# A hybrid attention layer: the gate chain moved into the output product, scores in half precision, the value projection in two pieces

## The reference

```python
u = rmsnorm(h, norm_g)
proj = u @ w_in            # gq 256, gk 256, gv 512, g_gate 512, g_low 16, sq 512, sk 128, sv 128, s_gate 512
z = g_low @ w_gate_up + b_gate
log_a = log_sigmoid(z) / 16
# gated linear attention, 4 heads (dk 64, dv 128): S_t = diag(exp(log_a_t)) S_{t-1} + k_t v_t^T ; o_t = q_t S_t
o_gla = rmsnorm(o, gla_norm)
# sliding-window attention: 8 heads, 2 key heads, width 64, window 128
s = (q . k) * 64**-0.5 ; p = softmax([s where in the window, sink])[:-1] ; o_swa = p @ v
y = concat(o_gla * silu(g_gate), o_swa * silu(s_gate)) @ w_out
h = h + y ; y_prompt = rmsnorm(h, norm_f)
```

## Time and profile before

| | |
|---|---|
| median of 3 runs | 963.65 us (963.21 to 964.19) |
| the profiled execution | 962.79 us, its span 960.8 us |
| granted PE clock over the span | 0.957 |
| PE busy | 889.7 us, 93% of the span |
| DVE, ACT, POOL busy | 72%, 42%, 6% |
| chain that ended last | PE 73%, DVE 21%, issue 2%, ACT 2% |

### The profile page before, as it was taken

The page is one execution under the profiler, slowest core; times in us unless marked ns, Lnnn a source line. Parts: engine busy times, 40 slices in busy tenths (PEclk is TensorE's granted clock), DMA queues, the critical chain, the costliest instruction groups (busy, mean ns, idle before and its releaser), DMA issues.

```text
span 960.8 us, 21676 instructions
## 1 busy us (share of the span) xinstructions
PE 889.7 (93%) x8701; PEld 618.8 (64%) x8701; DVE 689.4 (72%) x2140; ACT 399.4 (42%) x1096; POOL 57.6 (6%) x101
## 2 busy tenths in 40 slices
PE   1697699999999999999999999999999999999977
PEld 1673457585857666675758585766767575856755
DVE  5999858586776859495867678594959585776673
ACT  6885434343534243343434342434434343433311
POOL 0000101010101001010101010000101010101000
PEclk9798699999999999999999999999999999997776
DMA  9640102020202010010202020201102020101220
GB/s 381 249 166 0 67 1 89 1 90 1 89 1 89 2 66 24 23 67 2 89 1 90 1 89 2 89 1 42 49 4 86 1 89 1 48 2 45 78 113 24
DMA packets 15219, 56.47 MB, mean 59 GB/s; under 512 B 3569, under 2 KB 5001, under 8 KB 13840
## 3 DMA queue, kind: packets, MB, share of 16 engines
q1 hardware_dynamic: 14832, 55.02, 15.3%
q10 hardware_dynamic: 288, 0.07, 0.0%
HBM read 44.30 MB, written 10.78 MB: 57 GB/s over the span
## 4 chain that ended last, share of the span: by engine, by line
PE 73%; DVE 21%; issue 2%; ACT 2%; DMA 1%; SPq 0%; DVEq 0%
PE bank L511 19%; PE bank L512 19%; PE bank L513 19%; DVE flex L1404 4%; PE bank L661 3%; DVE bank L1398 2%; PE bank L595 2%; DVE flex L406 2%; PE bank L708 2%; PE bank L685 1%; PE bank L681 1%; DMA w_out_lo<-in_w 1%; DVE flex L1309 1%; PE bank L647 1%; DVE flex L405 1%
## 5 line engine op out<-in xcount | busy, mean ns | idle before, releaser
L511 PE MATMUL bank<-u_hi,w_in_hi_lo 128*128 128x128 f16 (+1 forms) x1288 | 208.8, 215 | 12.6 <-DVE w_in_hi_lo L1546 12.3
L512 PE MATMUL bank<-u_lo,w_in_hi_lo 128*128 128x128 f16 (+1 forms) x1288 | 208.4, 215 | 0.0
L513 PE MATMUL bank<-u_hi,w_in_hi_lo 128*128 128x128 f16 (+1 forms) x1288 | 208.4, 215 | 0.0
L511 PE MATMUL bank<-w_in_hi_lo,u_hi 128*128 128x512 f16 (+3 forms) x528 | 177.2, 344 | 0.8 <-issue 0.6
L512 PE MATMUL bank<-w_in_hi_lo,u_hi 128*128 128x512 f16 (+3 forms) x528 | 176.9, 343 | 0.0
L513 PE MATMUL bank<-w_in_hi_lo,u_lo 128*128 128x512 f16 (+3 forms) x528 | 176.8, 343 | 0.0
L511 PEld LDWEIGHTS bank<-u_hi,w_in_hi_lo 128*128 128x128 f16 x1288 | 124.2, 99 | 24.7 <-DVE w_in_hi_lo L1546 12.5
L512 PEld LDWEIGHTS bank<-u_lo,w_in_hi_lo 128*128 128x128 f16 x1288 | 124.2, 99 | 0.2
L513 PEld LDWEIGHTS bank<-u_hi,w_in_hi_lo 128*128 128x128 f16 x1288 | 124.2, 99 | 0.0
L511 PE MATMUL bank<-w_out_hi,ogT_hi 128*128 128x512 f16 x256 | 98.0, 383 | 0.0
L512 PE MATMUL bank<-w_out_lo,ogT_hi 128*128 128x512 f16 x256 | 97.9, 382 | 0.0
(11 more groups left out here) (263 smaller groups left out, 1765.3 us busy)
## 6 DMA issues: line engine op xcount, KB each, us to landing
xT<-in_xT SPq DMA_DIRECT2D x16, 512.0 KB, 4.5
x_rows<-in_xq SPq DMA_DIRECT2D x16, 512.0 KB
flex<-in_w SPq DMA_DIRECT2D x4, 2048.0 KB, 9.9
flex<-in_xq SPq DMA_DIRECT2D x16, 512.0 KB, 3.5
out_y<-flex SPq DMA_DIRECT2D x16, 512.0 KB, 2.6
w_out_lo<-in_w SPq DMA_DIRECT2D x2, 2048.0 KB, 9.9
w_out_hi<-in_w SPq DMA_DIRECT2D x1, 2048.0 KB, 10.2
w_out_hi<-in_w SPq DMA_DIRECT2D x1, 1088.0 KB, 7.2
```

Of the source, the lines that this page charges most:

```text
L511: nc.tensor.matmul(out, a_hi, b_hi, start=start and i == 0, stop=False)
L512: nc.tensor.matmul(out, a_hi, b_lo, start=False, stop=False)
L513: mm = nc.tensor.matmul(out, a_lo, b_hi, start=False, stop=stop and i == last)
```

## The change

1. The gate chain of the next tile (turn_low, gate_up, take_low, take_z, log_gate, sums, differences, decays, factors) is done in the body of the tile before. turn_low(t) and gate_up(t) in PE's body now serve tile t+1: turn_low stands after turn_keys, gate_up before gla_out. On DVE take_z follows take_gv, sums follow norm_x, factors stand between residual and final_norm. On ACT log_gate follows head_norm, decays stand after the gates and before split_u. Tile 0 has functions of its own at the start, in bank accS.
2. The scores are three half-precision products. ACT writes q's high half (take_sq), DVE the low half (a new take_sq, which now frees the bank), DVE both halves of k (take_kv, one operation more), all scaled by 2^-15; the scale of the scores moves into the constant `nsig` of row_max. The copy of k to the next tile's window copies both halves.
3. gv's projection is cut: four of its eight steps after sklow, four after leaf_scores. split_v moves behind sums.

The place of bc(t+2) is the same in both lists. The diff, cut to its core:

```diff
         tr = Ring(...
-                  [("glT", "act"), ("z", "dve"), ("pt0", "dve"), ("pt1", "dve"), ("pt2", "dve"), ("pt3", "dve"),
-                   ("KST", "act"), ("SU", "dve"), ("og0", "dve"), ("og1", "dve")])
+                  [("pt0", "dve"), ("pt1", "dve"), ("pt2", "dve"), ("pt3", "dve"), ("KST", "act"),
+                   ("glT", "act"), ("z", "dve"), ("SU", "dve"), ("og0", "dve"), ("og1", "dve")],
...
             def scores(t, pair):
                 for i in range(2):
-                    for h, name in enumerate(units):
-                        mm = nc.tensor.matmul(..., sq[r:r + HD, t.p, 2 * pair + i, :], kwin[r:r + HD, t.p, :],
-                                              start=True, stop=True)
+                    for step, (lq, lk) in enumerate(((0, 0), (0, 1), (1, 0))):
+                        for h, name in enumerate(units):
+                            mm = nc.tensor.matmul(..., q16[r:r + HD, t.p, lq, 2 * pair + i, :],
+                                                  k16[r:r + HD, t.p, lk, :], start=step == 0, stop=step == 2)
...
             def body(t):                      # PE
-                    turn_low(t)
                     proj(nxt, "gqk")
-                    gate_up(t)
                     scores(t, 0)
                     proj(nxt, "sq")
                 turn_probs(t, 0)
...
                 scores(t, 1)
                     proj(nxt, "sklow")
+                    proj(nxt, "gv", 4)
                 values(t, 0)
...
-                    proj(nxt, "gv")
+                    proj_rest(nxt, "gv", 4)
                 values(t, 2)
...
                 turn_keys(t)
+                turn_low(t)
                     proj(nxt, "gg", 3)
+                gate_up(t)
                 gla_out(t)
...
             def body(t):                      # ACT
-                    take_low(t)
                     take_qk(nxt)
-                log_gate(t)
                 probs(t, 0)
...
-                decays(t)
                 probs(t, 2)
...
                 take_kst(t)
+                take_low(t)
...
                 head_norm(t)
+                log_gate(nxt)
                 take_out(t, 0)
...
                 nc.scalar.preload_act_table_set(LOG_EXP_SET)
+                decays(nxt)
                     split_u(t + 2)
...
             def take_kv(t):                   # DVE
-                    V.tensor_scalar(kwin[:, t.p, P:2 * P], bank[:, 0:P], inv[:, 2:3], None, ALU.mult)
+                    V.tensor_scalar(k[:, 0, P:2 * P], bank[:, 0:P], V_UNIT, None, ALU.mult).then_inc(dve_k.sem, 1)
...
+                    V.scalar_tensor_tensor(out=k[:, 1, P:2 * P], in0=bank[:, 0:P], scalar=V_UNIT,
+                                           in1=k[:, 0, P:2 * P], op0=ALU.mult, op1=ALU.subtract)
...
+            def take_sq(t):
+                act_q.wait(dve, "qh", t)
+                V.scalar_tensor_tensor(out=q16[:, t.p, 1], in0=pj.bank("sq", t)..., scalar=V_UNIT,
+                                       in1=q16[:, t.p, 0], op0=ALU.mult, op1=ALU.subtract
+                                       ).then_inc(pj.freed["dve"], 1)
...
                 if i == 3:                    # DVE, start
...
+                    V.tensor_scalar(nsig[:, :], invq[:, 1:2], inv[:, 2:3], -1.0 / (V_UNIT * V_UNIT), ALU.mult, ALU.mult
+                                    ).then_inc(scored, 1)
+                    dve.wait_ge(scored, 1)
+                    V.tensor_scalar(nsig[:, :], nsig[:, :], -SCORE_FLOOR, None, ALU.min)
...
+                if i == 3:
+                    take_sq(Tile(0))
                 if i == 4:
+                    take_sq(Tile(1))
                     take_gv(Tile(0))
...
             def body(t):                      # DVE
-                    take_z(t)
                     row_max(t, 0)
                     row_max(t, 1)
-                sums(t)
+                    take_sq(nxt)
                 take_pt(t, 0)
...
-                factors(t)
                 take_pt(t, 2)
...
                     take_gv(nxt)
-                    split_v(nxt)
+                take_z(t)
...
                     norm_x(t + 2)
+                sums(nxt)
+                    split_v(nxt)
                     scale_u(t + 2)
                     split_u(t + 2)
                 residual(t)
+                factors(nxt)
                 final_norm(t)
...
+            differences(Tile(0))              # POOL
             def body(t):
-                differences(t)
                 gates_over_sums(t)
+                differences(t + 1)
```

More of the change, by code:

```diff
@@ L113, with __init__ @@
 class Ring:
-    def __init__(self, banks, full, freed, order, tail=None, head=None):
+    def __init__(self, banks, full, freed, order, tail=None, head=None, last=None):
         self.banks, self.full, self.freed, self.order = banks, full, freed, order
+        self.last = order if last is None else last
         self.tail = order if tail is None else tail
@@ L125, in _list @@
     def _list(self, t):
+        if t.static and t.off == NT - 1:
+            return self.last
         return self.tail if t.sample else self.order
@@ L610, in values @@
             def values(t, u):
[L611 to L612 removed]
+                if u == 0:
+                    if t.static and t.off == 0:
+                        pe.wait_ge(z_taken, 1)
+                    else:
+                        dve_o.wait(pe, "sg", t + -1)
                 if u == 0:
@@ L637, in gate_up, with first_turn_low, first_gate_up @@
                 mm.then_inc(tr.full, 1)
+            def first_turn_low():
+                pj.wait_freed(pe, "sklow", Tile(0))
+                nc.tensor.transpose(accS[0:RANK, 0:P], glow[:, 0, :], ident[:, :]).then_inc(low_turned, 1)
+            def first_gate_up():
+                pe.wait_ge(low_taken, 1)
+                for f in range(FT):
+                    mm = nc.tensor.matmul(accS[:, (f + 1) * P:(f + 2) * P], wgu[:, f * P:f * P + P], glT[:, :],
+                                          start=True, stop=True)
+                mm.then_inc(z_full, 1)
             def leaf_scores(t):
@@ L825, in _ @@
             proj(Tile(0), "gv")
-            turn_low(Tile(0))
+            first_turn_low()
             proj(Tile(1), "gv")
@@ L830, in _ @@
             pe.wait_ge(init, 1)
-            gate_up(Tile(0))
+            first_gate_up()
             scores(Tile(0), 0)
@@ L1734, in _ @@
                     dve.wait_ge(w_lo_done, i)
-                    take_z(Tile(0))
+                    first_take_z()
                     row_max(Tile(0), 0)
```

112 lines of the change are left out of this document (75 added, 37 removed).

## The result

The kernel after takes **952.43 us** (median of 4 runs, 950.77 to 952.50), the kernel before 963.76 on the same chip: ratio 0.9879, 95% interval 0.9862 to 0.9896. It is 1.2% faster, 6.2 us dearer than the 946.2 forecast, and inside the range of 941 to 956. The profiled execution took 952.36 us with a span of 950.6, so 1.8 us lie around the span, where it was 2.0 before.

The account below looks back on a forecast made before the run. PE was taken to bound the kernel, busy 51.57 of 52.29 us a tile. Bodies -19.3, start +3.4 and end -1.5 summed to -17.4, giving 946.2 us, range 941 to 956.

Parts of the forecast that it names:

- The gap: PE's wait for ACT's exponentials at transposes 2 and 3, bodies 1 to 14: closes, -0.93 x 14 = -13.0 us.
- The scores: A call of twelve half-precision products, heads side by side: 0.80 us, -0.27 a call, 28 times, -7.6 us.
- The first rival: No overlap of the two heads in float16 scores: a call takes 1.43 us, total 964; chance 10%.
- The switches: Changes in the number of rows between PE's products: one more a tile at 0.09 us, +1.3 us.
- (b): Row maxima 0 and 1 behind factors: probabilities fit by 0.2 us, costed nothing; T is the tile's start on PE.
- second rival: Exponentials late again, at the first transposes: 0.5 x 14 = 7 us, total 953; chance 15%.
- (a): u for the tile after next, across DVE, POOL and ACT: ready T+49.9, wanted T+50.9, covered by 1.0 us.
- (c), (d): Leaf bank freed T+23.0, wanted T+23.4; take_z holding DVE until gate_up ends, T+28.7: both costed at nothing.
- The start: Before tile 1: gv(1) waiting for take_sq(1) behind row_bound(6), +2.75, and body 0, +0.65: +3.4 us.
- The end: Tile 15, gate chain already done: 12.9 us to the second scores' end against 14.5; -1.5 us (0 to -3).
- u late: u not ready, PE stalls at gqk: slower kernel from 2.2 us beyond the margin, 974 at 3 us; chance 6%.
- All at the low bounds: Scores at 0.64 us a call and a cheaper start: 940 us; chance 3%.

Follow-up runs that it names:

- gs: The changed kernel with gv's projection whole again, where it stood before (gate chain and half-precision scores kept): 972.80 us, ratio 1.0095.
- v_only: The kernel before with only gv's projection of the next tile split, twelve products between second scores and first values: 960.47 us, ratio 0.9970.
- g_only: The kernel before with only the next tile's gate chain moved ahead of gla_out, scores in float32, gv's projection whole: 963.81 us, ratio 1.0004.
- const_scale: early_sq with row_max multiplying by the constant -1.0 in place of the per-partition scale: 944.46 us, ratio 0.9807.
- early_sq: The changed kernel with take_sq(Tile(1)) on DVE moved ahead of row_bound(6), right behind lo_w(4): 947.05 us, ratio 0.9832.
- bound_first: The changed kernel with two calls of the start swapped on PE, bound(6) ahead of gv(1): 951.25 us, ratio 0.9875.
- warm: early_sq with useless half-precision products in two PE waits of the first body, fourteen before the first values, nine before turn_out: 945.06 us, ratio 0.9807.
- heads_apart: The changed kernel with the scores' loops swapped, three products of head 0 in a row, then three of head 1: 951.30 us, ratio 0.9877.
- heads_far: early_sq with all six score products of head 0 ahead of all six of head 1: 950.89 us, ratio 0.9871.

## Why the prediction was right in its range and 6 us off

- **The gap.** Right. -0.93 a tile was forecast; -0.90 is seen at transposes 2 and 3 and -0.07 at the values products ahead of them. No wait of PE is listed from 140 to 863 us. gs (+20 us without the split) shows that gv's twelve products are the cover, v_only that the split alone only moves the wait, and g_only that sums() out of the way is not enough either. Both parts are needed, as the forecast had them together.
- **The scores.** Right in mechanism: 0.76 a call against 0.80, and 1.41 with the overlap taken away against a bound of 1.43. The first rival, no overlap in float16, is refuted.
- **The switches** were read from one side only. A change in the number of rows takes 0.09 us ahead of the first product with the new number, which is what the prediction read. If that product is a float32 one, about 0.10 more pass behind it. Two places in the tile show what the moved chain adds, first after, then before (lines 658 and 715 are gate_up and gla_out; line 681 is gla_out before):

```profile
480.17 0.38 PE L527 MATMUL bank<-w_in_hi_lo,u_hi 128*128 128x512 f16 x1
...
482.21 0.71 PE L658 MATMUL bank<-g_lowT,w_gate_up 16*128 16x128 f32 x4
482.84 1.13 PE L715 MATMUL bank<-gla_state,flex 128*128 128x256 f32 x4
483.81 0.27 PE L719 MATMUL bank<-gla_v,flex 128*128 128x128 f32 x1
```

```profile
481.45 0.38 PE L511 MATMUL bank<-w_in_hi_lo,u_hi 128*128 128x512 f16 x1
...
483.39 1.03 PE L681 MATMUL bank<-gla_state,flex 128*128 128x256 f32 x4
484.26 0.27 PE L685 MATMUL bank<-gla_v,flex 128*128 128x128 f32 x1
```

The nine products ahead of gate_up take 2.04 us and not 1.94, gla_out's first four records 0.97 and not 0.87: +0.20 a tile, 2.8 us in all, where +0.09 and 1.3 us were forecast. g_only has the same two differences. With this the tile adds up: 0.97 of the gap and 2 x 0.31 of the scores, less 0.09 lost at (b) and 0.20 here, is 1.30, and 1.30 was measured.
- **Luck in the bodies.** -18.1 against -19.3 looks closer than the terms are: the gap and the scores earned some 1.5 us more than forecast, the switches and (b) cost 2.7 us more.
- **Margin (b)**, the exponentials of units 0 and 1, forecast to fit by 0.2 us, misses by 0.09. Row_max started on time (462.50, T+8.2), but unit 1's transpose starts at 466.14, T+11.9, where its probabilities were to be there at T+11.7; PE, a little faster by the scores, would have been ready at T+11.8. Row_max's new operand, 0.06 us on each of four operations ahead of that point, was costed at nothing, and const_scale shows that it alone decides: 1.2 us in all. So the second rival came true for 1.2 of its 7 us, and one of the prediction's own signs of a wrong mechanism, transposes 0 and 1 waiting for exponentials, was met, in small.
- **Margins (a), (c), (d).** Nothing listed. (a) kept 0.88 us of its 1.0; scale_u started 0.5 us further behind the broadcast than before (500.85 behind 499.87, and 500.81 behind 500.31), where 0.3 was forecast.
- **The start failed.** It was put at +3.4 us with bounds of +1 and +4.5, and measured +8.6. The mechanism, gv(1) held by take_sq(1) behind row_bound(6), was named rightly, and early_sq shows it to be 4.1 us of start by itself. Mis-sized were three terms. The wait of PE is 3.55 us, not 3.0. It was then costed through DVE, whose waits were to give back 0.35; bound_first shows that PE's list is what binds, and nothing came back. And the clock was left out: 1.60 us of slow gv(1) and 1.64 us of slow sg, 3.2 of the 5.2 us missing. Both stand behind idle stretches of PE, one of which the prediction itself had made 3 us long. The rest is body 0 up to gla_out, 1.12 instead of 0.65, of which 0.50 came on the path over DVE and ACT and was costed at nothing (which of its operations make it was not tried), and the 0.62 us of clock ahead of this point. That last part moves between kernels that have the same PE list up to there: turn_low(0) starts at 69.34 in after, 68.75 in early_sq, 68.73 in bound_first and 69.36 in warm. So some 0.6 us of the start's miss goes with the place of the slow stretch and not with the work of the change.
- **The end** was -1.5 and is -0.7. From the last tile's first product to the end of the second scores it took 862.45 to 876.31 = 13.9 us, where 12.9 was forecast and 14.5 measured before: the transposes took 1.85 us and the second scores 1.39, at the lower clock. Two other kernels tell the list from the clock. warm has after's list there and took 13.0 us, with the transposes at 1.59 and the second scores at 0.76; v_only has before's list and took 12.95. The stretch in before, v_only, after and warm, with the granted clock as the last number but two:

```profile
871.96:886.43 14.47, 14.04 (x266) 11.89 (x264) 11.22 (x37) 6.81 (x25) 2.52 (x5) 0.65 0.20 75
...
871.50:884.45 12.95, 12.52 (x266) 10.86 (x264) 10.67 (x36) 6.38 (x24) 2.52 (x5) 0.74 0.23 84
...
862.45:876.31 13.86, 12.21 (x270) 10.17 (x268) 11.38 (x37) 4.47 (x17) 0.00 (x0) 0.71 0.20 70
...
856.72:869.70 12.98, 11.32 (x270) 9.98 (x268) 10.53 (x34) 4.47 (x17) 0.00 (x0) 0.74 0.16 51
```

So 12.9 was reckoned rightly for such a clock, but it was set against 14.5 us that had more of the lower clock in them. From list to list these runs show between nothing (v_only and warm) and 0.6 us (before and after) for the end, and not 1.5. Nor can they give the whole end to 1 us: in the five kernels with after's ending (after, early_sq, bound_first, gs, warm) it goes from 86.4 to 88.1, and v_only's is 2.2 us shorter than before's with the same work.
- **The other rivals.** u late did not occur: no wait of PE is listed at gqk. All at the low bounds did not either: a call took 0.76 us and not 0.64, and the start was dearer and not cheaper.

## What to carry to other kernels

Cost a wait on PE twice: by its length, and by the products that may follow it at 1.2 GHz, here 1.6 us behind one of 3.55. When two kernels differ by 1 or 2 us, look first at where the lower clock lies in each: here one unchanged ending took 88.8 and 86.6 us. Where one engine frees a bank that another engine's list is about to use, put that small operation ahead of the long one beside it: 0.7 us of DVE moved by 3.4 us was worth 4.1 us, over a third of what the whole change earned. And test a change of several parts by leaving each out: here one part alone cost 34 us and one brought nothing, and together with the third they earned 11.

## What the runs showed of the hardware

- Half-precision products on rows 0-63 and 64-127 run side by side, and they need not be neighbours in the list: with three places between them a call took 0.77 us, with six 0.99, and all in one half 1.41. The Trainium skill (TensorE: Matmul & The Clock Gate, "Part 3: Packing small matmuls") has the concurrency, and says that matmuls keep strictly to the order of the list; the measured calls, and the starts within 0.04 us of one another in heads_apart and heads_far, speak against the second for products in different halves of the rows, and the measurement decides.
- The same idle stretch of 2.37 us at the same place was followed by products of 0.38 us in one kernel and of 0.63 in another. Filling it took the slow ones away.
- A change in the number of rows between neighbouring products cost 0.2 us in all: 0.09 ahead of the first product with the new number and 0.10 behind it, if it is a float32 one (gate_up between gg's products and gla_out: 2.04 us for 1.94, and 0.97 for 0.87).
- With the same work and the same idle time of PE, the stretch from tile 15 on took 88.8 us at a mean granted clock of 0.71 and 86.6 at 0.74 (before and v_only).
- The custom row-maximum operation of 128 columns takes 343 ns with a constant scale and 405 ns with a scale read per partition.
